# Two of the four weight sums of an FFN pair on GpSimd, joined remainders and re-cut parts in a fast-matrix-product FFN

## The chip, the cores and the metric

The kernel runs on one core of a Trainium2 chip. A core has five engines that run side by side and meet at semaphores: TensorE (PE in the profile; its weight loads are PEld), VectorE (DVE), ScalarE (ACT), GpSimd (POOL) and SyncE (SP), which here starts nearly all transfers. The time is the device time of the whole program in microseconds (us); lower is better.

## The reference, cut to what matters

Two decoder layers run over 1024 prompt tokens and 64 sample tokens (T = 1088), model width 1024. Each layer has three kinds of sequence mixing, an output projection, and the feed-forward part (FFN) that the change is about:

```python
mix = jnp.concatenate([o_gla, o_lru, o_mla], axis=-1) @ w_out
x = _layer_norm(DEEPNORM_ALPHA * x + gate1 * mix, ln1_g, ln1_b)
h2 = x * (1 + scale2) + shift2
g_ff, u_ff = jnp.split(h2 @ ffn_w_gu, 2, axis=-1)     # 1024 -> 2 x 2816
f = (jax.nn.silu(g_ff) * u_ff) @ ffn_w_down           # 2816 -> 1024
x = _layer_norm(DEEPNORM_ALPHA * x + gate2 * f, ln2_g, ln2_b)
```

Everything is float32.

## The kernel before, in words

The kernel is one launch; each stage has an instruction stream for every engine, and the order in each stream is written out by hand (no scheduler moves anything). `stage_out_ffn` holds the output projection, both layer norms and the FFN; it runs once per layer.

**Three passes.** TensorE multiplies in a rounded float32 form. Each operand is split into a rounded part ("hi", cast by ScalarE) and a remainder ("lo" = raw minus hi, subtracted by VectorE), and each product is made of three passes: hi by hi, hi by lo, lo by hi (`three_passes`, lines 434 to 436).

**Pairs and seven products.** A pair `m` is 128 gate and 128 up columns of `w_gu` for one half of the tokens. There are 22 such column blocks and two token halves (512 tokens as 2 x 256, then 576 as 2 x 288), so 44 pairs per layer. A pair is a 2 x 2 block product (two halves of the contraction, two halves of the tokens), made in seven block products instead of eight. For this a weight set has seven slots of 128x512: slots 0, 2, 4 and 5 are loaded by SyncE (`pair_in`, four transfers), and slots 3, 2, 1 and 6 are filled, in this order, by four sums (`w_sum`, lines 2512 to 2525, all on VectorE): slot3 = slot2 + slot5; slot2 = slot0 - slot2; slot1 = slot3 - slot0; slot6 = slot4 - slot1. Two sets take turns. The load of slot s of set m waits until product s of pair m-2 is done. Products go to four PSUM banks in turn (0 to 3); VectorE combines the seven results (`step` in the vector block, lines 2571 to 2625) into gate and up values, ScalarE applies silu, and VectorE multiplies.

**Rounding.** ScalarE rounds slot by slot into a ring of six (`w_rounded`, L2338); VectorE takes the remainder slot by slot, in place (`w_rest`, L2530), five products ahead of TensorE (`LO_AT`). TensorE waits for the remainder before each product.

**Parts.** `FPART` cuts the 22 blocks of a token half into eight parts of two or three pairs, so 16 parts (0 to 15) per layer. After the pairs of a part come its down products (`down`): 8 units of 512 tokens in the first token half, 16 units of 288 in the second, in PSUM banks 4 to 7. A unit sums over the pairs of the part. The first few units (`first`: 2 in the first token half, 4 in the second) are started without the part's last pair; then TensorE waits for the last pair's activations (`s_ul`, line 2253), finishes these units, does the transposes of a layer norm that were hung on this part (`norms_beside`), and then the other units. VectorE adds each unit to the residual stream (L420), takes the remainders of the down weights (L2536), and in the middle of the down phase makes the four sums of one pair ahead (`SUMS_IN_D`) and some remainders (`LO_D`).

The activations of a part's last pair pass a chain over two engines: VectorE adds the last product (L2603), ScalarE applies silu (L2408), VectorE multiplies (L2554), ScalarE rounds (L2353), VectorE takes the remainder (L2548). Its VectorE links stand in one queue with the down weights' remainders and all the rest.

**The last part.** Its down weights come in one transfer, `w_tail` (L2170), which lands in the room of weight set 0 and so waits for all products of the last but one pair. SyncE's queue is in order: for each pair m of a part it issues `pair_in(m + 2)`, and the wait for `w_tail` stands after the pairs of part 14. Part 15 before is the pairs 41, 42 and 43:

```python
for q in range(NQ):
    for m in range(*PAIRS[q]):
        if m + 2 < NPAIR:
            pair_in(m + 2)
    ...
    if q == NQ - 2:
        sp.wait_ge(s_pp, 7 * (NPAIR - 1))
        src = a["w_down"][bass.ds(layer[0], 1), :, :, NF - 3:NF]
        sp.dma_start(WLR, ...).then_inc(s_wt, 16)
```

GpSimd does nothing in this stage.

Of the kernel before, what the change touches and what calls it, by code (L numbers as in the profile page):

```python
# [27 lines left out]
P = 128  # L28
# [94 lines left out]
def build(nc, a, out, n_phys):  # L123
    ctx = ExitStack()
    with ctx:
# [1857 lines left out]
        FPART = [(0, 2), (2, 5), (5, 8), (8, 11), (11, 14), (14, 17), (17, 19), (19, 22)]  # L1983
# [11 lines left out]
        nh, nl = 5, 4  # L1995
        for q, (m0, m1) in enumerate(PAIRS):
            ends = (7 * m1 + 4, 7 * m1 + 2, 7 * m1 + NR) if q < NQ - 1 else (7 * m1,) * 3
            for j in range(7 * m0, 7 * m1):
                h, l_ = max(nh, min(j + 7, ends[0])), max(nl, min(j + 6, ends[1]))
                HI_AT[j], LO_AT[j] = range(nh, h), range(nl, l_)  # L2000
                nh, nl = h, l_
            HI_D[q], LO_D[q] = range(nh, ends[2]), range(nl, ends[2])
            nh = nl = ends[2]
# [22 lines left out]
        WLH = at("w_tail_hi", o, [P, KD, 3, P])  # L2026
# [4 lines left out]
        WLR, WLL = (at("w_tail" + x, r1 + 10 * 4 * 288 * 4, [P, KD, 3, P]) for x in ("", "_lo"))  # L2031
        assert o <= end and o_wo >= r1 + KD * T * 4
        o = o_small
        P1T, U2T, U3T, C22T = (at(x, o + 1152 * i, [P, 288]) for i, x in enumerate(
            ("ffn_p1", "ffn_u2", "ffn_u3", "ffn_c22")))
# [51 lines left out]
        def stage_out_ffn():  # L2087
# [9 lines left out]
            s_ws, s_wh, s_wl = (sem(x) for x in ("w_ffn_sums", "w_ffn_rounded", "w_ffn_rest"))  # L2097
            s_pp, s_p1, s_sa, s_sb = (sem(x) for x in ("ffn_product_done", "p1_kept", "silu_0_done", "silu_1_done"))
            s_u2, s_u3, s_c22, s_u5, s_c11, s_c21, s_c12 = (sem(x) for x in (
                "u2_ready", "u3_ready", "c22_ready", "u5_ready", "c11_ready", "c21_ready", "c12_ready"))  # L2100
            bank_read = (s_p1, s_u2, s_u3, s_u5, s_c11, s_c21, s_c12)
# [21 lines left out]
            with nc.Block() as block:  # L2123
                @block.sync
                def _(sp):
# [33 lines left out]
                    for q in range(NQ):  # L2159
# [18 lines left out]
                def _(pe):  # L2178
# [49 lines left out]
                    def down(q):  # L2228
                        m0, m1 = PAIRS[q]
                        last, first = m1 - m0 - 1, 2 * NU[q] // KD if q < NQ - 1 else 4  # L2230
# [16 lines left out]
                        for u in range(first):  # L2247
# [62 lines left out]
                def _(act):  # L2310
# [17 lines left out]
                    def w_rounded(j):  # L2328
                        m, i = divmod(j, 7)
                        if i in (0, 4, 5):  # L2330
                            act.wait_ge(s_set[m % 2], 64 * (m // 2 + 1))
                        else:
                            act.wait_ge(s_ws, 4 * m + {3: 1, 2: 2, 1: 3, 6: 4}[i])
# [141 lines left out]

                @block.vector
                def _(dve):
# [34 lines left out]
                    def w_sum(m, p):  # L2512
                        w = WGR[:, m % 2]
                        if p == 1:
                            dve.wait_ge(s_set[m % 2], 64 * (m // 2 + 1))
                            ins = dve.tensor_tensor(w[:, 3], w[:, 2], w[:, 5], ALU.add)  # L2516
                        if p == 2:
                            ins = dve.tensor_tensor(w[:, 2], w[:, 0], w[:, 2], ALU.subtract)  # L2518
                        if p == 3:
                            dve.wait_ge(s_ws, 4 * m + 1)  # L2520
                            ins = dve.tensor_tensor(w[:, 1], w[:, 3], w[:, 0], ALU.subtract)  # L2521
                        if p == 4:
                            dve.wait_ge(s_ws, 4 * m + 3)
# [3 lines left out]
                    def w_rest(j):  # L2527
                        m, i = divmod(j, 7)
                        dve.wait_ge(s_wh, j + 1)
                        dve.tensor_tensor(WGL[:, m % 2, i].bitcast(F32R), WGR[:, m % 2, i], WGH[:, (j + 1) % NR],  # L2530
                                          ALU.subtract).then_inc(s_wl, 1)
# [12 lines left out]
                    def act_rest(m, h):  # L2544
# [4 lines left out]
                                          ALU.subtract).then_inc(s_ul, 1)  # L2549

# [20 lines left out]
                    def step(m, i):  # L2571
# [5 lines left out]
                        u1, u2, u3, c22 = (v[:, 0:w] for v in (P1T, U2T, U3T, C22T))  # L2577
# [4 lines left out]
                        if i == 1:  # L2582
# [4 lines left out]
                            if m > m0:  # L2587
                                act_rest(m - 1, 0)
                                act_rest(m - 1, 1)
# [426 lines left out]
```

## Time and profile before

| | us |
|---|---|
| median of 3 runs (lowest, highest) | 3690.62 (3680.36, 3694.93) |
| profiled execution | 3688.22 |
| its span, first to last instruction | 3686.4 |
| TensorE busy | 3321.2 (90%) |
| VectorE busy | 2378.9 (65%) |
| ScalarE busy | 1538.3 (42%) |
| GpSimd busy | 193.7 (5%) |

The profile is of one execution. The time is 1.8 us more than the span (start and end outside the first and last instruction). "Idle before" and the arrow name how long an engine stood still before an instruction and what released it. A busy share is an average over stages with different limits, so the waits are read stage by stage. PEclk is the granted TensorE clock: 1.00 is 2.4 GHz, 0.50 is 1.2 GHz, and a value between is a stretch with some of both.

### The profile page before, as it was taken

Reading aid. Unit: us, or ns where it says so; the run is one execution under the profiler, and the core shown is the slowest. Engines: PE = TensorE matmul, PEld = TensorE weight load, DVE = VectorE, ACT = ScalarE, POOL = GpSimd, SP = SyncE. Lnnn points to the kernel's source line nnn. Section 1 sums busy time; section 2 is a strip of 40 time slices with the busy share of each in tenths; the row PEclk is TensorE's granted clock in tenths of the full one; section 3 lists DMA queues with packets and bytes.
Section 4 is the critical chain, followed back from the end, with each engine's and each line's share of the span. In section 5 each row is a group of like instructions: output and inputs, shape, how many; then the busy total and the mean of one; then the engine's idle time right before and its main releaser. Section 6 shows DMA issues by size and latency. Waiting matters only on the chain. (4 is left out here: it accounts for less than half of the span.)

```text
span 3686.4 us, 61020 instructions
## 1 busy us (share of the span) xinstructions
PE 3321.2 (90%) x23548; PEld 2773.6 (75%) x23548; DVE 2378.9 (65%) x4902; ACT 1538.3 (42%) x3093; POOL 193.7 (5%) x252
## 2 busy tenths in 40 slices
PE   6987899998989998999789869999989999989996
PEld 5864566666988888999779546666668888789996
DVE  5146664444688879888642466644447877898886
ACT  5235554443344444453231545634424444544331
POOL 0011111110000000000000121011100000000000
PEclk9987998998999999999989869999989999999998
DMA  5144003442123322222111500044312332222221
GB/s 205 31 151 144 22 1 134 153 161 58 48 84 89 90 86 75 83 85 87 36 51 29 190 29 1 1 182 162 115 46 65 90 95 81 83 79 87 84 93 55
DMA packets 157570, 316.86 MB, mean 86 GB/s; under 512 B 18491, under 2 KB 85341, under 8 KB 146406
## 3 DMA queue, kind: packets, MB, share of 16 engines
q1 hardware_dynamic: 145766, 229.08, 20.1%
q0 software_dynamic: 11520, 83.89, 6.4%
q8 instruction: 191, 3.13, 0.4%
q14 instruction: 93, 0.76, 0.1%
HBM read 306.41 MB, written 6.51 MB: 85 GB/s over the span
## 5 line engine op out<-in xcount | busy, mean ns | idle before, releaser
L2338 ACT CAST w_ffn_hi<-w_ffn 128x512 fp32r<-128x512 f32 x616 | 367.8, 617 | 312.8 <-DVE w_ffn L2521 183.1
L434 PE MATMUL psum<-ffn_act_hi,w_down_hi 128*128 128x288 f32 (+1 forms) x960 | 335.8, 350 | 104.5 <-DVE ffn_act_lo L2548 86.6
L2530 DVE TENSOR_TENSOR w_ffn_lo<-w_ffn,w_ffn_hi 128x512 fp32r<-128x512 f32 x616 | 415.0, 682 | 7.5 <-ACT w_ffn_hi L2338 5.8
L435 PE MATMUL psum<-h_lo,w_ffn_hi 128*128 128x256 f32 (+1 forms) x1408 | 408.7, 290 | 0.0
L434 PE MATMUL psum<-h_forms_hi,w_ffn_hi 128*128 128x288 f32 x1232 | 366.1, 297 | 29.0 <-DVE ffn_u L2596 29.0
L436 PE MATMUL psum<-h_forms_hi,w_ffn_lo 128*128 128x288 f32 x1232 | 365.7, 297 | 0.0
L420 DVE SCALAR_TENSOR_TENSOR xT<-psum,adaT,xT 128x512 f32<-128x512 f32 (+3 forms) x432 | 236.4, 567 | 199.5 <-PE psum L436 199.0
L434 PE MATMUL psum<-h_hi,w_ffn_hi 128*128 128x256 f32 x1232 | 348.3, 283 | 4.3 <-DVE xT L427 1.9
L436 PE MATMUL psum<-h_hi,w_ffn_lo 128*128 128x256 f32 x1232 | 347.9, 282 | 0.0
L436 PE MATMUL psum<-ffn_act_hi,w_down_lo 128*128 128x288 f32 (+1 forms) x960 | 329.3, 343 | 0.0
L435 PE MATMUL psum<-ffn_act_lo,w_down_hi 128*128 128x288 f32 (+1 forms) x960 | 328.5, 342 | 0.0
L434 PEld LDWEIGHTS psum<-ffn_act_hi,w_down_hi 128*128 128x128 f32 x960 | 188.2, 196 | 133.7 <-DVE ffn_act_lo L2548 96.6
L435 PEld LDWEIGHTS psum<-h_lo,w_ffn_hi 128*128 128x128 f32 x1408 | 267.3, 190 | 0.7
L434 PEld LDWEIGHTS psum<-h_forms_hi,w_ffn_hi 128*128 128x128 f32 x1232 | 233.5, 190 | 30.0 <-DVE ffn_u L2596 29.9
L434 PEld LDWEIGHTS psum<-h_hi,w_ffn_hi 128*128 128x128 f32 x1232 | 235.2, 191 | 6.7 <-DVE xT L427 2.3
L436 PEld LDWEIGHTS psum<-h_hi,w_ffn_lo 128*128 128x128 f32 x1232 | 235.1, 191 | 0.0
L436 PEld LDWEIGHTS psum<-h_forms_hi,w_ffn_lo 128*128 128x128 f32 x1232 | 233.6, 190 | 0.0
L436 PEld LDWEIGHTS psum<-ffn_act_hi,w_down_lo 128*128 128x128 f32 x960 | 188.2, 196 | 16.4
L435 PEld LDWEIGHTS psum<-ffn_act_lo,w_down_hi 128*128 128x128 f32 x960 | 188.5, 196 | 13.1
L1883 ACT COPY keysT<-psum 128x512 f32<-128x512 f32 x192 | 106.8, 589 | 202.2 <-PE psum L1793 195.6
L1937 DVE TENSOR_REDUCE dec_max<-psum 128x1 f32<-128x1024 f32 x64 | 78.3, 1224 | 170.3 <-PE psum L1809 170.3
L1663 DVE TENSOR_REDUCE mla_neg_max<-psum 128x1 f32<-128x128 f32 (+7 forms) x128 | 96.7, 756 | 92.8 <-PE psum L1487 92.0
(436 smaller groups left out, 7631.9 us busy)
## 6 DMA issues: line engine op xcount, KB each, us to landing
w_ffn<-in_w_gu SPq DMA_DIRECT2D x352, 256.0 KB, 2.6
w_ada_pair<-in_w_ada SPq DMA_DIRECT2D x40, 1024.0 KB, 5.2
w_down<-in_w_down SPq DMA_DIRECT2D x176, 192.0 KB, 2.4
w_ada_first<-in_w_ada SPq DMA_DIRECT2D x4, 2048.0 KB, 22.0
w_out<-in_w_out SPq DMA_DIRECT2D x16, 512.0 KB, 7.3
w_down<-in_w_down SPq DMA_DIRECT2D x64, 128.0 KB, 2.1
w_in_T<-in_w_in_T SPq DMA_DIRECT2D x12, 512.0 KB, 4.3
z<-in_x_prompt SPq DMA_DIRECT2D x8, 512.0 KB, 6.9
```

The source lines that it names most:

```text
L420: ins = eng.scalar_tensor_tensor(XT[:, c, t0:t0 + wp], ps[:, 0:wp], ADA[:, gate + c, 0:1], XT[:, c, t0:t0 + wp], ALU.mult, ALU.add)
L434: pe.matmul(o, wh, xh, start=first, stop=False)
L435: pe.matmul(o, wh, xl, start=False, stop=False)
L436: return pe.matmul(o, wl, xh, start=False, stop=last)
L1663: dve.tensor_reduce(NM[:, i % 2:i % 2 + 1], bank(2 * (i % 2), 2)[:, 0:scores_item(i)], AX.X, ALU.max, negate=True).then_inc(s_mx, 1)
L1883: copy(dst, src).then_inc(done, 1)
L1937: lk(dve.tensor_reduce(MXD[:, s % 2, :], bank(3, 2), AX.X, ALU.max))
L2338: act.copy(WGH[:, (j + 1) % NR].bitcast(F32R), WGR[:, m % 2, i]).then_inc(s_wh, 1)
L2530: dve.tensor_tensor(WGL[:, m % 2, i].bitcast(F32R), WGR[:, m % 2, i], WGH[:, (j + 1) % NR], ALU.subtract).then_inc(s_wl, 1)
```

## The change

1. **GpSimd takes two of the four sums.** A new GpSimd block makes slot 3 and then slot 2 of every pair as soon as its set has landed; VectorE keeps slots 1 and 6 at their old places.
2. **Joined remainders.** `w_rest` takes two neighbouring slots in one instruction where the ring allows: a pair's seven remainders are four instructions (`LO_GROUPS`), one product later than before. The two halves of an activation's remainder are one instruction (`acts_rest`), except for a part's last pair; two of the seven combining additions are one instruction of twice the width.
3. **Four first units** in every part, where the first token half had two.
4. **The norm's transposes** stand before the wait for the last pair's activations instead of after it.
5. **Parts are cut anew**: the last two of a token half are (17, 20), (20, 22) instead of (17, 19), (19, 22). `w_tail` is for two pairs instead of three.

```diff
-        FPART = [(0, 2), (2, 5), (5, 8), (8, 11), (11, 14), (14, 17), (17, 19), (19, 22)]
+        FPART = [(0, 2), (2, 5), (5, 8), (8, 11), (11, 14), (14, 17), (17, 20), (20, 22)]
...
-        nh, nl = 5, 4
+        LO_GROUPS = [(7 * m + i, 2 if i + 1 + m % 2 < 7 and (i or m % 2) else 1) for m in range(NPAIR)
+                     for i in ((0, 2, 4, 6) if m % 2 else (0, 1, 3, 5))]
+        LO_GROUPS = [(j, min(n, 7 - j % 7)) for j, n in LO_GROUPS]
+        nh, nl = 5, 3
...
-            ends = (7 * m1 + 4, 7 * m1 + 2, 7 * m1 + NR) if q < NQ - 1 else (7 * m1,) * 3
+            ends = (7 * m1 + 4, 7 * m1 + 1, 7 * m1 + NR) if q < NQ - 1 else (7 * m1,) * 3
...
+                while nl < len(LO_GROUPS) and LO_GROUPS[nl][0] < min(j + 5, ends[1]):
+                    nl += 1
+                LO_AT[j] = LO_GROUPS[l0:nl]
...
-                            src = a["w_down"][bass.ds(layer[0], 1), :, :, NF - 3:NF]
+                            src = a["w_down"][bass.ds(layer[0], 1), :, :, NF - 2:NF]
...
-                        last, first = m1 - m0 - 1, 2 * NU[q] // KD if q < NQ - 1 else 4
+                        last, first = m1 - m0 - 1, 4
...
+                        norms_beside(q)
                         pe.wait_ge(s_ul, 2 * m1)
                         for u in range(first):
                             part(u, last).then_inc(s_dn, 1)
-                        norms_beside(q)
...
+                @block.gpsimd
+                def _(pool):
+                    for m in range(NPAIR):
+                        w = WGR[:, m % 2]
+                        pool.wait_ge(s_set[m % 2], 64 * (m // 2 + 1))
+                        pool.tensor_tensor(w[:, 3], w[:, 2], w[:, 5], ALU.add).then_inc(s_wp, 1)
+                        pool.wait_ge(s_wp, 2 * m + 1)
+                        pool.tensor_tensor(w[:, 2], w[:, 0], w[:, 2], ALU.subtract).then_inc(s_wp, 1)
...
                     def w_sum(m, p):
                         w = WGR[:, m % 2]
-                        if p == 1:
-                            dve.wait_ge(s_set[m % 2], 64 * (m // 2 + 1))
-                            ins = dve.tensor_tensor(w[:, 3], w[:, 2], w[:, 5], ALU.add)
-                        if p == 2:
-                            ins = dve.tensor_tensor(w[:, 2], w[:, 0], w[:, 2], ALU.subtract)
                         if p == 3:
-                            dve.wait_ge(s_ws, 4 * m + 1)
+                            dve.wait_ge(s_wp, 2 * m + 1)
                             ins = dve.tensor_tensor(w[:, 1], w[:, 3], w[:, 0], ALU.subtract)
...
-                    def w_rest(j):
+                    def w_rest(j, n):
                         m, i = divmod(j, 7)
-                        dve.wait_ge(s_wh, j + 1)
...
+                        r = (j + 1) % NR
+                        dve.wait_ge(s_wh, j + n)
+                        dve.wait_ge(s_wp, 2 * m + 2)
+                        if i <= 1 < i + n or i <= 4 < i + n:
+                            dve.wait_ge(s_ws, 2 * m + 2)
+                        dve.tensor_tensor(WGL[:, m % 2, i:i + n].bitcast(F32R), WGR[:, m % 2, i:i + n], WGH[:, r:r + n],
+                                          ALU.subtract).then_inc(s_wl, n)
...
+                    def acts_rest(m):
...
+                        dve.tensor_tensor(UL[:, f, v].bitcast(F32R), UR[:, f, v], UH[:, f, v], ALU.subtract).then_inc(s_ul, 2)
...
-                            dve.tensor_tensor(c22, p, u3, ALU.add).then_inc(s_c22, 1)
-                            dve.tensor_tensor(u2, p, u2, ALU.add).then_inc(s_u5, 1)
+                            dve.tensor_tensor(UTS[:, 2:4, 0:w], p.unsqueeze(1).to_broadcast([P, 2, w]), UTS[:, 1:4:2, 0:w],
+                                              ALU.add).then_inc(s_c22, 1)
```

## Rows read from the trace of the kernel before

**Rows 1.** The page: busy us, share of the span, instructions; granted clock in 40 slices.
```profile
PE 3321.2 (90%) x23548; PEld 2773.6 (75%) x23548; DVE 2378.9 (65%) x4902; ACT 1538.3 (42%) x3093; POOL 193.7 (5%) x252
PEclk9987998998999999999989869999989999999998
```

**Rows 2.** TensorE's waits: engine line <- releaser: us in total, times, longest.
```profile
PE psum L434 <- DVE ffn_act_lo L2548: 88.8, 32, 4.8
PE psum L434 <- DVE ffn_u L2596: 30.3, 6, 13.4
PE psum L434 <- DVE xT L420: 12.9, 9, 2.2
```

**Rows 3.** Timelines of SP, DVE and PE near layer 0's end: start, us, instruction [idle before].
```profile
1792.10 0.38 SPq L2170 DMA_DIRECT2D w_tail<-in_w_down  x1
1792.53 2.15 SPq L2135 DMA_DIRECT2D w_ffn<-in_w_gu  x4
...
1801.42 0.69 DVE L2516 TENSOR_TENSOR w_ffn<-w_ffn 128x512 f32<-128x512 f32 x1 [15.13 <-DMA w_ffn<-in_w_gu]
...
1805.43 0.61 PE L434 MATMUL psum<-h_forms_hi,w_ffn_hi 128*128 128x288 f32 x1 [13.36 <-DVE ffn_u L2596]
```

**Rows 4.** Stretches: us, busy (instructions) of PE, PEld, DVE, ACT, POOL, clock, DMA.
```profile
1805.40:1809.00 3.60, 3.57 (x15) 3.57 (x16) 3.55 (x8) 2.18 (x5) 0.00 (x0) 0.50 0.00 0
1809.00:1813.00 4.00, 4.00 (x26) 4.00 (x26) 3.13 (x8) 3.12 (x6) 0.00 (x0) 0.80 0.00 0
...
1077.10:1082.10 5.00, 4.96 (x24) 4.26 (x25) 2.52 (x4) 0.82 (x1) 0.00 (x0) 0.69 0.26 79
...
1287.90:1292.90 5.00, 5.00 (x18) 3.14 (x18) 1.50 (x2) 1.50 (x3) 0.00 (x0) 0.66 0.28 79
...
1601.80:1605.40 3.60, 3.60 (x30) 3.60 (x31) 2.37 (x8) 1.29 (x2) 0.00 (x0) 1.00 0.29 78
```

**Rows 5.** PE's timeline: first unit and end of the wait, parts 4 and 12.
```profile
1228.32 0.40 PE L434 MATMUL psum<-ffn_act_hi,w_down_hi 128*128 128x512 f32 x1
...
1234.37 0.80 PE L434 MATMUL psum<-ffn_act_hi,w_down_hi 128*128 128x512 f32 x1 [3.14 <-DVE ffn_act_lo L2548]
...
1653.07 0.29 PE L434 MATMUL psum<-ffn_act_hi,w_down_hi 128*128 128x288 f32 x1
...
1658.10 0.40 PE L434 MATMUL psum<-ffn_act_hi,w_down_hi 128*128 128x288 f32 x1 [1.68 <-DVE ffn_act_lo L2548]
```

**Rows 6.** DVE's timeline in part 4: its last long idle time, the chain's last link.
```profile
1211.42 0.42 DVE L2586 TENSOR_TENSOR ffn_u<-psum,ffn_p 128x256 f32<-128x256 f32 x1 [0.80 <-PE psum L436]
1211.76 0.75 DVE L2548 TENSOR_TENSOR ffn_act_lo<-ffn_act,ffn_act_hi 128x256 fp32r<-128x256 f32 x2
...
1233.88 0.43 DVE L2548 TENSOR_TENSOR ffn_act_lo<-ffn_act,ffn_act_hi 128x256 fp32r<-128x256 f32 x1 [0.47 <-ACT ffn_act_hi L2353]
```

**Rows 7.** DVE's groups by form: shapes, count | busy us, mean ns | idle before.
```profile
L2530 DVE TENSOR_TENSOR w_ffn_lo<-w_ffn,w_ffn_hi 128x512 fp32r<-128x512 f32 x616 | 415.0, 682 | 7.5 <-ACT w_ffn_hi L2338 5.8
L2672 DVE TENSOR_TENSOR w_out_lo<-w_out,w_out_hi 128x1024 fp32r<-128x1024 f32 x16 | 19.5, 1218 | 11.0 <-ACT w_out_hi L2421 11.0
L2586 DVE TENSOR_TENSOR ffn_u<-psum,ffn_p 128x256 f32<-128x256 f32 x44 | 18.5, 421 | 29.5 <-PE psum L436 29.5
```

**Rows 8.** GpSimd's additions by line: ns min/median/max; then timelines of POOL and DVE.
```profile
L855 POOL TENSOR_TENSOR hT<-lru_i,hT x4: 2491/2512/2535, 252.9 to 2077.6; 128x1088 f32<-128x1088 f32 x4
L860 POOL TENSOR_TENSOR gv_gg<-gv_gg,gla_norm_g x8: 1389/1395/1850, 334.7 to 2154.9; 128x576 f32<-128x576 f32 x8
...
338.80 1.84 POOL L860 TENSOR_TENSOR gv_gg<-gv_gg,gla_norm_g 128x576 f32<-128x576 f32 x1
...
338.20 1.18 DVE L1206 TENSOR_TENSOR gla_sample_states<-gla_sample_states,gla_chunk_decay 128x512 f32<-128x512 f32 x1 [4.60 <-ACT gla_state_blocks L1052]
339.41 0.69 DVE L1207 TENSOR_TENSOR gla_sample_states<-gla_sample_states,psum 128x512 f32<-128x512 f32 x1
```

**Rows 9.** The page's DMA issues: KB each, median us to landing.
```profile
w_ffn<-in_w_gu SPq DMA_DIRECT2D x352, 256.0 KB, 2.6
```

**Rows 10.** The tile w_tail: DVE's row (ns min/median/max), and its landing.
```profile
L2542 DVE TENSOR_TENSOR w_tail_lo<-w_tail,w_tail_hi x4: 1748/1749/1751, 1816.4 to 3638.2; 128x1536 fp32r<-128x1536 f32 x4
...
DMA to landing us min/median/max: 6.6/6.6/6.6
```

**Rows 11.** PE's timeline: the first product of layer 0's pair 23.
```profile
1414.39 0.40 PE L434 MATMUL psum<-h_forms_hi,w_ffn_hi 128*128 128x288 f32 x1 [1.16 <-DVE ffn_u L2596]
```

More of the change, by code:

```diff
@@ L1994, in build @@
         HI_AT, LO_AT, HI_D, LO_D = {}, {}, {}, {}
-        nh, nl = 5, 4
+        LO_GROUPS = [(7 * m + i, 2 if i + 1 + m % 2 < 7 and (i or m % 2) else 1) for m in range(NPAIR)
+                     for i in ((0, 2, 4, 6) if m % 2 else (0, 1, 3, 5))]
+        LO_GROUPS = [(j, min(n, 7 - j % 7)) for j, n in LO_GROUPS]
+        nh, nl = 5, 3
         for q, (m0, m1) in enumerate(PAIRS):
-            ends = (7 * m1 + 4, 7 * m1 + 2, 7 * m1 + NR) if q < NQ - 1 else (7 * m1,) * 3
+            ends = (7 * m1 + 4, 7 * m1 + 1, 7 * m1 + NR) if q < NQ - 1 else (7 * m1,) * 3
             for j in range(7 * m0, 7 * m1):
[L1999 to L2003, printed above, removed]
+                h = max(nh, min(j + 7, ends[0]))
+                HI_AT[j], nh = range(nh, h), h
+                l0 = nl
+                while nl < len(LO_GROUPS) and LO_GROUPS[nl][0] < min(j + 5, ends[1]):
+                    nl += 1
+                LO_AT[j] = LO_GROUPS[l0:nl]
+            l0 = nl
+            while nl < len(LO_GROUPS) and sum(LO_GROUPS[nl]) <= ends[2]:
+                nl += 1
+            HI_D[q], LO_D[q] = range(nh, ends[2]), LO_GROUPS[l0:nl]
+            nh = ends[2]
         SUMS_IN_D = [q for q in range(NQ - 1) if q != NQ // 2 - 1]
@@ L2030, in build @@
         UH = at("ffn_act_hi", o, [P, 3, NB1]); o += 3 * NB1 * 4
-        WLR, WLL = (at("w_tail" + x, r1 + 10 * 4 * 288 * 4, [P, KD, 3, P]) for x in ("", "_lo"))
+        WLR, WLL = (at("w_tail" + x, r1 + 10 * 4 * 288 * 4, [P, KD, 2, P]) for x in ("", "_lo"))
         assert o <= end and o_wo >= r1 + KD * T * 4
         o = o_small
-        P1T, U2T, U3T, C22T = (at(x, o + 1152 * i, [P, 288]) for i, x in enumerate(
-            ("ffn_p1", "ffn_u2", "ffn_u3", "ffn_c22")))
+        UTS = at("ffn_u", o, [P, 4, 288])
+        P1T, U3T, C22T, U2T = (UTS[:, i] for i in range(4))
         assert o + 5 * 1152 <= r1
@@ L2576, in step @@
                         p = bank(j % 4)[:, 0:w]
-                        u1, u2, u3, c22 = (v[:, 0:w] for v in (P1T, U2T, U3T, C22T))
+                        u1, u2, u3 = (v[:, 0:w] for v in (P1T, U2T, U3T))
                         if i == 0 and m > m0:
@@ L2587, in step @@
                             if m > m0:
[L2588 to L2589 removed]
+                                acts_rest(m - 1)
                         if i == 2:
@@ L2700, in _ @@
                         if u == 13:
-                            for p in range(1, 5):
-                                w_sum(0, p)
+                            w_sum(0, 3)
+                            w_sum(0, 4)
                         if u in (14, 15):
-                            w_rest(2 * (u - 14))
-                            w_rest(2 * (u - 14) + 1)
+                            w_rest(*LO_GROUPS[u - 14])
                     form_rest(0, 4)
+                    w_rest(*LO_GROUPS[2])
                     form_rest(0, 5)
```

40 lines of the change are left out of this document (21 added, 19 removed).

## The prediction, as it stood before the changed kernel ran

> **What bounds the kernel now.** I read the page first: TensorE is busy for 3321 of 3686 us [rows 1], so the change can win only TensorE's idle time in the FFN and what the slower clock behind idle time costs. Next the waits of TensorE [rows 2]: 88.8 us in 32 waits for the remainder of the activations (L2548), one per part, and 30.3 us in 6 waits for L2596, of which one is 13.4 us. That one I followed through the queues near the end of layer 0 [rows 3]. SyncE issues `w_tail` at 1792.10 and only then the four loads of pair 43: its queue is in order, and the wait for pair 42's last product stands ahead of them. VectorE stands 15.13 us for that set, TensorE 13.36 us. The 6 waits for L2596 hold this one twice (26.7 us). After it the clock is 0.50 for 3.6 us and 0.80 for 4.0 us [rows 4]: 0.50 x 3.6 + 0.20 x 4.0 = 2.6 us of work lost.
>
> The other waits are one per part. In part 4 the down phase begins at 1228.32 and TensorE stands 3.14 us until 1234.37 [rows 5], 6.05 us after the start. I call this distance the chain. Its length is VectorE's backlog: VectorE has its last long idle time before 1211.42 and works almost without a break until the last remainder at 1233.88 [rows 6]. Behind a 3.1 us wait the clock reads 0.69 and 0.66 over 5 us [rows 4] (parts 1 and 5, first and last of five alike ones), some 1.7 us of work lost each. In part 12 the chain is 5.03 us and the wait 1.68 us [rows 5]; behind a wait of that size the clock stays 1.00 [rows 4].
>
> **The tail order.** The new cut makes part 14 the pairs 39 to 41, so `pair_in(43)` is queued ahead of the wait for `w_tail`. This takes away 13.4 + 2.6 = 16.0 us per layer. `w_tail` now has one pair (11.2 us; seven products of 1.6) to land and be split in. It took 6.6 us to land beside four loads with 1.5 MB [rows 10], is now 1 MB, and its two remainders shrink from 1.75 us to 1.22, the row for 128x1024 [rows 7, 10]. It fits. But the last part has two pairs: its early units hold one pair instead of two, and cover about 1.7 us less of a chain that is 4.2 us today and perhaps 3.5 then. I give back 1.0 us. Part 14, with two pairs, stands 2.6 and 1.1 us today; with three it becomes like part 12: I take 1.9 saved. Sum 16.9 us per layer.
>
> **What VectorE loses and gains.** In its stream an instruction starts some 0.08 us before its predecessor's record ends, so 128x512 costs 0.60, 128x1024 1.14 and 128x256 0.33 us [rows 7]. Two sums less: 1.20 us per pair. Three joined remainders: 3 x 0.07; joined additions and activation remainders: 0.07 each. Together 1.55 us per pair. The middle and the last pair of a part decide the backlog: 3.1 us, and one remainder is due later.
>
> Against it stands GpSimd. No row shows its sum at 128x512; 1088 columns take 2.51 and 576 take 1.39 us [rows 8], so 2.2 ns per column and 1.25 us for 512 by that line (an estimate; ends 0.6, VectorE's own pace, and 2.5, the long row). The two engines also stand in each other's way: VectorE's L1206 of 128x512 with both inputs in SBUF took 1.18 us beside a GpSimd addition, not the 0.68 of such a form, and the GpSimd addition that overlapped it took 1.84 instead of 1.39; L1207 with an input in PSUM took 0.69 at the same time [rows 7, 8]. So one seems to wait until the other's whole instruction is done, unless VectorE reads PSUM.
>
> The Trainium skill says the same (SBUF — State Buffer, the overview of its two sides): the pair of ports is an exclusive lock, held for the whole instruction, against VectorE operations with two SBUF inputs. It speaks against this change; the trace agrees in the three rows named.
>
> When does it strike? Set m+1's last load is issued when product 5 of pair m-1 is done, 1.4 us before that pair's end, and lands 2.6 us later [rows 9]: 1.3 us into pair m, and for a part's last pair 1.3 us into the chain. GpSimd then runs 1.25 us, takes its own semaphore, and runs 1.25 us again. About 74% of VectorE's stream has two SBUF inputs, so each addition holds it 0.9 us or so, at worst 1.25. I laid the stream of the middle and last pair of part 4 out instruction by instruction. Middle pair: 1.3 us held (VectorE idles at first), its last addition ends 0.3 us earlier than today. Last pair: 2.1 us held. In the chain: two more, 2.1 us. Sum +5.5 - 3.1 - about 0.8 for remainders moved or not due = +1.5: the chain becomes 7.5 us instead of 6.05. The ends: 4.0 if GpSimd costs nothing, 9.5 if its additions hold VectorE longer.
>
> **Four first units and transposes ahead.** In the first token half two units with two pairs cover 2.9 us (1228.32 to 1231.23); four cover 5.8 us. The transposes ahead add 1.0 to 2.9 us (8 to 16 of them; parts 0 to 6 have some). Parts 1 to 5 cover 6.9 to 8.7 us against a chain of 7.5: the wait goes and with it the slow clock, 3.14 + 1.7 = 4.8 us each. What is late next is a remainder: slot 6 of an odd last pair now stands behind the sums of the next set and ends about 0.5 us after TensorE could use it. I keep 0.8 us: 5 x 4.0 = 20.0 us per layer. The other early units' conditions (a free bank, the split down weights) come in time: VectorE idles 7 us of part 3's down phase today, and has 1.35 us less to do there.
>
> Part 0 covers 5 to 6 us of a chain of 6.4 today: of 4.8 + 1.9 us waits and 2 us of slow clock 3.0 are saved. Parts 6 and 7: part 6 becomes like part 5. Part 7 has now two pairs, and behind it VectorE forms the block sums of the next token half, some 29 us without a break from the chain's end to pair 23's start at 1414.39 [rows 11]. VectorE sets this stretch, so down work moved out of it (5.8 us of TensorE) moves from under cover to the open. Its chain is about 7.8 us (7.4 today) with 2.9 covered. Part 6's wait of 3.3 us and slow clock of 3.1 gained, this lost, 1.8 us gained on VectorE: 3.7 us saved in both.
>
> **Second token half.** There first is four already. Part 12 covers 3.35 us; laid out the same way, the chain goes from 5.0 to 5.7 us, the wait from 1.7 to 2.4: 0.7 us lost each in parts 12 and 13. Parts 9 to 11 have transposes (1.0 to 1.9 us) as new cover: 1.0 us won each; in layer 1 VectorE is without a break after the chain, and it is the two sums less (1.2 us) that win it. Part 8: nothing, a longer chain against 2 us more cover. Together +1.6 us.
>
> **Sum.** 16.9 + 20.0 + 3.0 + 3.7 + 1.6 = 45.2 us per layer, 90.4 in both. The profiled execution took 3688.2: 3597.8. It lies 2.4 us under the median of the runs shown, so I forecast **3600 us** (-2.4%).
>
> **The rivals.**
> *GpSimd's additions hold VectorE about 2 us per part longer than laid out* (chain 9.5 us). For it: in each later pair both sets of instructions want the same ports, and 1.25 us is a line through two points. Against: the rows show waits of 0.5 us, never a pile. Parts 1 to 5 then stand 1 to 2.5 us, some clock lost: 12 of 20 us gone; parts 0, 6, 7: 4; second half, seven parts x 1.4: 10. Per layer 45 - 26 = 19: 3600 + 52 = 3652. Chance 0.20.
> *GpSimd costs VectorE hardly anything* (it slips into idle time or PSUM reads, chain 4 to 5 us). Then the second half's waits fall to about 0.5 us and parts 0 and 7 win 1.5 each: 11 us more per layer, 3578. Chance 0.14.
> *`w_tail` comes late now.* It has half the cover it had. If ScalarE stands in its queue for it and the chain of the last part waits behind, 5 us per layer: 3610. For it: ScalarE's rounding of it comes at product 3, 6.4 us after the issue, and 6.6 is the landing. Chance 0.10.
> *Slower than before*: VectorE is the pace of every pair. Per pair of 10.0 us it has 8.2 + 0.8 (down weights) and two holds. If one holds it 2.5 us, the upper end, its stream is 14 us and TensorE waits in the products too (for L2530 and L2592), in every part. It decides from 3 us plus clock in each of 15 parts, 45 us per layer, which is where a hold costs some 1.6 us instead of 0.9. At 1.25 us more each of six holds per part adds 7.5 us less 3 of cover or slack, 15 parts, two layers, 135 us: 3735. Chance 0.03.
> The forecast itself has 0.53.
>
> **How the numbers follow.** The tail order alone is worth 32 us and rests on one queue. The low end takes the cheap GpSimd and a little (3574), the high end the expensive one (3655); what lies outside is part of the 0.03, the tails of the two and some error of my layout, under 0.2. The likeliest case alone spans 3585 to 3620. A measurement of this kernel tells about 0.5% (18 us) from nothing. Faster 0.94, the same 0.03, slower 0.03.
>
> **What would show it.** TensorE's 13.4 us wait for L2596 is gone in both layers, and SyncE issues pair 43's loads ahead of `w_tail`. The wait for L2548 falls from 88.8 to about 40 us, all of it in parts 0, 7 and the second half; behind parts 1 to 5 the clock reads 1.00. GpSimd has 176 additions of 1.25 us where alone and up to 2.4 beside VectorE; some L2530-like rows of VectorE have maxima 1.2 us above their median, those reading PSUM do not. The prediction is wrong if TensorE waits for the remainders inside the products, if GpSimd's additions take well over 2 us each, or if the waits in parts 1 to 5 only became shorter.

## The result, and the profile after

| | before | changed |
|---|---|---|
| median, lowest and highest (us) | 3690.84 (3680.36, 3694.93) | 3651.02 (3644.46, 3654.12) |
| profiled execution | 3688.2 | 3649.7 |

Four executions of each. The ratio is 0.9894, with a 95% interval of 0.9869 to 0.9919: the change wins 1.1%, some 39 us, where 90 were forecast (2.4%). The time lies near the top of the range and on the first rival's figure (3652).

The page of the changed kernel, busy time and granted clock; it answers to [rows 1]:

```profile
PE 3309.3 (91%) x23548; PEld 2760.5 (76%) x23548; DVE 2384.5 (65%) x4318; ACT 1542.5 (42%) x3093; POOL 463.2 (13%) x428
PEclk9997999998999999999989969999989999999998
```

VectorE has 584 instructions fewer than before and lost two sums per pair, yet it is busy for 5.6 us more. That is the first sign of the cost.

TensorE's waits, to be read beside [rows 2] (waited-for line, us in total, times, longest):

```profile
PE psum L434 <- DVE ffn_act_lo L2565: 34.9, 16, 3.6
PE psum L434 <- DVE w_down_lo L2553: 23.9, 12, 3.3
PE psum L434 <- DVE w_ffn_lo L2547: 20.9, 36, 1.1
...
PE psum L434 <- DVE xT L420: 8.5, 10, 2.3
PE psum L308 <- DVE ffn_u L2626: 7.6, 4, 2.9
PE psum L256 <- DVE ffn_u L2626: 6.0, 4, 2.4
PE psum L319 <- DVE ffn_u L2626: 3.6, 3, 1.9
```

The two waits of 13.4 us for the last pair's first combination are gone, and the activations' wait fell from 88.8 to 34.9 us. Three kinds are new or far larger: down-weight remainders (4.9 us before, all in 4 waits), pair-weight remainders inside the products (none before), and the norm's transposes, which now stand ahead of the activations' wait and themselves wait for VectorE's last addition (17.2 us; none before). [rows 2] and the 4.9 us make 137 us; the seven rows above make 105. In the old places 88.6 us were won (53.9, 30.3 and 4.4), and 57.1 of them came back as 20.9 + 19.0 + 17.2 in the three new ones.

The chain in part 12, the place of [rows 5]'s last two rows: timelines of PE, POOL and DVE (start, us, instruction, idle before).

```profile
1644.55 0.30 PE L434 MATMUL psum<-ffn_act_hi,w_down_hi 128*128 128x288 f32 x1
...
1651.23 0.40 PE L434 MATMUL psum<-ffn_act_hi,w_down_hi 128*128 128x288 f32 x1 [3.33 <-DVE ffn_act_lo L2565]
```

```profile
1645.28 1.66 POOL L2490 TENSOR_TENSOR w_ffn<-w_ffn 128x512 f32<-128x512 f32 x1 [9.11 <-DMA w_ffn<-in_w_gu]
1647.02 1.38 POOL L2492 TENSOR_TENSOR w_ffn<-w_ffn 128x512 f32<-128x512 f32 x1
```

```profile
1645.71 0.45 DVE L2623 TENSOR_TENSOR ffn_u<-psum,ffn_u 128x288 f32<-128x288 f32 x1
1646.26 1.00 DVE L2637 TENSOR_TENSOR ffn_act<-ffn_u 128x288 f32<-128x288 f32 x1
1647.18 1.63 DVE L2553 TENSOR_TENSOR w_down_lo<-w_down,w_down_hi 128x384 fp32r<-128x384 f32 x1
1648.73 0.45 DVE L2626 TENSOR_TENSOR ffn_u<-psum,ffn_u 128x288 f32<-128x288 f32 x1
...
1650.71 0.46 DVE L2565 TENSOR_TENSOR ffn_act_lo<-ffn_act,ffn_act_hi 128x288 fp32r<-128x288 f32 x1 [0.50 <-ACT ffn_act_hi L2362]
```

The chain is 6.68 us, not 5.03. GpSimd's two additions fall into it. Each holds one VectorE instruction that reads two SBUF tensors: L2637 takes 1.00 where the same shape at L2577 takes 0.46, and a down-weight remainder takes 1.63 where it takes 0.55 just before. The additions with an input in PSUM (L2623, L2626) keep their 0.45. Behind the wait the clock is no longer 1.00 [rows 4], while in parts 2 to 5, where the wait is gone or short, it now is. In part 1 it is not: TensorE stands 2.75 us for a down weight there, and the clock behind that reads 0.66 (stretches in parts 12, 1, 2 and 4; the columns of [rows 4]):

```profile
1651.20:1655.20 4.00, 3.97 (x21) 3.97 (x22) 2.38 (x8) 0.46 (x1) 0.00 (x0) 0.67 0.33 88
1085.30:1090.30 5.00, 5.00 (x15) 3.96 (x16) 4.68 (x8) 2.27 (x5) 0.00 (x0) 0.66 0.06 10
1130.40:1135.40 5.00, 5.00 (x26) 4.04 (x25) 2.77 (x5) 2.69 (x7) 0.00 (x0) 1.00 0.40 110
1230.20:1235.20 5.00, 4.99 (x21) 3.87 (x21) 3.56 (x8) 1.47 (x3) 0.00 (x0) 1.00 0.53 154
```

All instructions of the stage show the same selection: weight remainders, GpSimd's two lines, one combining addition and one activation product (ns min/median/max).

```profile
L2547 DVE TENSOR_TENSOR w_ffn_lo<-w_ffn,w_ffn_hi x352: 677/1215/2345, 991.9 to 3598.2; 128x1024 fp32r<-128x1024 f32 x132, 128x512 fp32r<-128x512 f32 x44
L2490 POOL TENSOR_TENSOR w_ffn<-w_ffn x88: 1268/1360/2332, 981.1 to 3558.6; 128x512 f32<-128x512 f32 x88
L2492 POOL TENSOR_TENSOR w_ffn<-w_ffn x88: 1291/1393/2306, 983.0 to 3560.0; 128x512 f32<-128x512 f32 x88
...
L2609 DVE TENSOR_TENSOR ffn_u<-psum,ffn_u x88: 410/434/460, 1001.5 to 3596.2; 128x256 f32<-128x256 f32 x44, 128x288 f32<-128x288 f32 x44
...
L2577 DVE TENSOR_TENSOR ffn_act<-ffn_u x88: 412/459/1589, 1012.9 to 3605.7; 128x256 f32<-128x256 f32 x44, 128x288 f32<-128x288 f32 x44
```

The added time is in the maxima; L2609, which reads PSUM, has none.

### The profile page after: what moved, and what is told of

Read it like the earlier page. It is cut to its first block and busy times, and to the rows that moved or that the text cites. A ratio compares the mean times of both kernels' runs of the same rounds, so it can differ in the third digit from the quotient of the medians.

```text
span 3647.9 us, 61284 instructions
## 1 busy us (share of the span) xinstructions
PE 3309.3 (91%) x23548; PEld 2760.5 (76%) x23548; DVE 2384.5 (65%) x4318; ACT 1542.5 (42%) x3093; POOL 463.2 (13%) x428
## 5 line engine op out<-in xcount | busy, mean ns | idle before, releaser
L2547 DVE TENSOR_TENSOR w_ffn_lo<-w_ffn,w_ffn_hi 128x1024 fp32r<-128x1024 f32 (+1 forms) x352 | 409.4, 1163 | 15.6 <-issue 11.9
L434 PE MATMUL psum<-ffn_act_hi,w_down_hi 128*128 128x288 f32 (+1 forms) x992 | 344.5, 347 | 64.1 <-DVE ffn_act_lo L2565 31.7
L436 PE MATMUL psum<-ffn_act_hi,w_down_lo 128*128 128x288 f32 (+1 forms) x992 | 337.7, 340 | 0.0
L435 PE MATMUL psum<-ffn_act_lo,w_down_hi 128*128 128x288 f32 (+1 forms) x992 | 337.3, 340 | 0.0
L2490 POOL TENSOR_TENSOR w_ffn<-w_ffn 128x512 f32<-128x512 f32 x88 | 129.8, 1475 | 1585.3 <-DMA w_ffn<-in_w_gu 1585.3
L434 PEld LDWEIGHTS psum<-ffn_act_hi,w_down_hi 128*128 128x128 f32 x992 | 196.0, 198 | 91.6 <-DVE ffn_act_lo L2565 36.7
L435 PEld LDWEIGHTS psum<-ffn_act_lo,w_down_hi 128*128 128x128 f32 x992 | 196.3, 198 | 13.5
```

The costliest lines, as they stand in the source:

```text
L434: pe.matmul(o, wh, xh, start=first, stop=False)
L435: pe.matmul(o, wh, xl, start=False, stop=False)
L436: return pe.matmul(o, wl, xh, start=False, stop=last)
L2490: pool.tensor_tensor(w[:, 3], w[:, 2], w[:, 5], ALU.add).then_inc(s_wp, 1)
L2547: dve.tensor_tensor(WGL[:, m % 2, i:i + n].bitcast(F32R), WGR[:, m % 2, i:i + n], WGH[:, r:r + n], ALU.subtract).then_inc(s_wl, n)
```

## The experiments

Kernels of one group ran on one chip beside the kernel before (its medians: 3689.67, 3689.65, 3685.16). Ratios are against it, with 95% intervals; differences between two experiments are differences of medians, and I call one resolved only where the ratios' intervals are apart. The changed kernel ran in a session of its own, and the base of the second group (3617.70) is a kernel of the first, so where chips differ the ratios are the better measure.

### First group: which part of the change wins, which costs

**All four sums back on VectorE, the rest as changed.**

```diff
-  @block.gpsimd ...
+  if p == 1: dve.tensor_tensor(w[:, 3], w[:, 2], w[:, 5], ALU.add)
+  if p == 2: dve.tensor_tensor(w[:, 2], w[:, 0], w[:, 2], ALU.subtract)
```

> The change with all four sums back on VectorE at their old places; joined remainders, four first units, transposes ahead and the new cut stay. Theory H (holds): in the changed kernel GpSimd's additions hold VectorE 0.8 us each, three pairs of them fall into the chain of each part, and only two pairs of sums leave it. Then the chain of part 12 falls from 6.6 by 3 x 1.6 and rises by 2 x 1.2, to about 4.3 us, its wait from 3.3 to about 1.0, and the kernel is faster than the changed one: 3610 to 3625 us. Rival R (relief): taking two sums off VectorE is worth its price and what was lost is due to the joined, later remainders and the four first units; then this is slower than the changed kernel, 3660 us or more, and the waits inside the products grow.

Measured: 3621.56 (3620.54 to 3625.18), 0.9823 (0.9806 to 0.9839). Faster than the change, by 29 us: in this kernel the two sums are worth more on VectorE than on GpSimd where the change starts them. The time is as expected, its path only in part: part 12 waits 1.85 us, not 1.0, and its chain is 5.19 us, not 4.3. Only the pair of holds inside the chain shows in its length, not three pairs.

```profile
PE 3296.2 (91%) x23548; PEld 2747.5 (76%) x23548; DVE 2350.5 (65%) x4494; ACT 1542.4 (43%) x3093; POOL 194.1 (5%) x252
```

This line gives the price of a hold. VectorE has 176 instructions more than in the changed kernel, its lines 2525 and 2528:

```profile
L2525 DVE TENSOR_TENSOR w_ffn<-w_ffn x88: 679/682/689, 991.2 to 3545.3; 128x512 f32<-128x512 f32 x88
L2528 DVE TENSOR_TENSOR w_ffn<-w_ffn x88: 682/684/690, 991.8 to 3545.9; 128x512 f32<-128x512 f32 x88
```

A record is 0.68 us long but starts 0.08 us before the one ahead of it ends, so in VectorE's stream a sum costs 0.60 us, by the prediction's own reading: 106 us for the 176. Without them VectorE would be busy for 2245 us; with GpSimd's additions beside it, it is busy for 2384.5: 140 us for 176 additions, **0.79 us each**. The longer means of the stretched rows, shape by shape, add up to about the same (136 us). So moving a sum cost VectorE 0.19 us more than it saved, 34 us in all.

**The new cut alone**, on the kernel before.

```diff
-  (14, 17), (17, 19), (19, 22)]      w_tail: 3 pairs
+  (14, 17), (17, 20), (20, 22)]      w_tail: 2 pairs
```

> The kernel before with nothing but the new cut of the parts (17, 20), (20, 22) and the last transfer for two pairs. Both theories: the 13.4 us wait of each layer and the slow clock behind it go (32 us), part 7 and the last part cover less: 3658 to 3664 us. If the gain of the whole change over the kernel before (40 us) is nearly all this, the other edits together brought less than 10 us.

Measured: 3662.89 (3660.33 to 3667.34), 0.9933 (0.9916 to 0.9949): 27 us, two thirds of what the whole change wins. The 13 us waits are gone, the activations' wait is not touched:

```profile
PE psum L434 <- DVE ffn_act_lo L2548: 90.5, 32, 5.8
...
PE psum L434 <- DVE ffn_u L2596: 4.0, 4, 1.4
```

**GpSimd's sums alone**, on the kernel before (the GpSimd block of the diff, VectorE keeps slots 1 and 6, remainders slot by slot).

> The kernel before with nothing but two of the four sums on GpSimd. Theory H: each part's chain grows by 3 x 1.6 - 2 x 1.2 = 2.4 us, uncovered here, in some 30 parts, and the slow clock comes into the second token half: 60 to 100 us slower than before, 3750 to 3790. Rival R: the chain shrinks by 1 to 2 us, 30 to 50 us faster, 3640 to 3660.

Measured: 3749.36 (3741.27 to 3758.57), 1.0160 (1.0142 to 1.0177): 60 us **slower**, at the low end of what was expected. Alone, this part of the change is a loss:

```profile
PE psum L434 <- DVE ffn_act_lo L2555: 138.2, 32, 6.0
```

The same 32 waits as before, 1.5 us longer each, where 2.4 was expected. In the full change the same additions cost 29 us (the experiment above), about half; that the cut and the longer cover hide the rest is my reading, no run separates it.

**GpSimd's sums after the chain.** In a part's down phase GpSimd waits until the last pair's activations are done.

```diff
   pool.wait_ge(s_set[m % 2], 64 * (m // 2 + 1))
+  if m - 1 in [m1 for _, m1 in PAIRS[:-1]]:
+      pool.wait_ge(s_ul, 2 * (m - 1))
```

> The changed kernel, but GpSimd waits, for the set that lands during a part's chain, until the chain's last link is done. Theory H: one pair of holds (1.6 us) leaves the chain of every part and falls into the down phase where VectorE has slack: part 12 waits 1.7 instead of 3.3 us, the slow clock behind it goes; 20 to 35 us faster than the changed kernel, 3615 to 3630. Rival R: no change within 8 us, or slower where the down phase is VectorE's.

Measured: 3617.70 (3609.91 to 3621.22), 0.9813 (0.9797 to 0.9830): 33 us faster than the change. One wait per part gives back what GpSimd cost, and VectorE is busy for 2349.8 us, no longer than with the sums at home (2350.5). Part 12 shows what left the chain:

```profile
1629.80 0.29 PE L434 MATMUL psum<-ffn_act_hi,w_down_hi 128*128 128x288 f32 x1
...
1634.97 0.40 PE L434 MATMUL psum<-ffn_act_hi,w_down_hi 128*128 128x288 f32 x1 [1.82 <-DVE ffn_act_lo L2567]
```

The chain is 5.17 us, and the clock over the 4 us behind the wait reads 1.00 again. Against all four sums on VectorE the intervals overlap: on its own, GpSimd's help is worth nothing that these runs can tell. The remaining waits:

```profile
PE psum L434 <- DVE ffn_act_lo L2567: 22.4, 14, 2.6
PE psum L434 <- DVE w_down_lo L2555: 22.1, 12, 3.3
PE psum L434 <- DVE w_ffn_lo L2549: 21.2, 37, 1.1
```

The activations' wait fell by a third, and the other two did not move. So GpSimd is not their cause; the second group asks for it, with this kernel as its base.

### Second group: the waits that GpSimd does not explain

The pair-weight wait has two forms. Layer 0 has 20 of them. Seven are for a single remainder, slot 6 of an odd pair. DVE and PE in part 2 of the changed kernel:

```profile
1121.07 0.68 DVE L2534 TENSOR_TENSOR w_ffn<-w_ffn 128x512 f32<-128x512 f32 x1
1121.78 0.69 DVE L2537 TENSOR_TENSOR w_ffn<-w_ffn 128x512 f32<-128x512 f32 x1
1122.39 0.69 DVE L2547 TENSOR_TENSOR w_ffn_lo<-w_ffn,w_ffn_hi 128x512 fp32r<-128x512 f32 x1
```

```profile
1123.22 0.36 PE L434 MATMUL psum<-h_hi,w_ffn_hi 128*128 128x256 f32 x1 [0.60 <-DVE w_ffn_lo L2547]
```

The remainder that TensorE needs stands behind the next pair's two sums, of which nothing is due. These seven waits are 0.25 to 0.60 us. The other thirteen are for joined remainders, up to 1.12 us, and in twelve of them a held instruction stands just ahead in VectorE's queue. The same part, 3 us earlier:

```profile
1115.32 1.51 DVE L2637 TENSOR_TENSOR ffn_act<-ffn_u 128x256 f32<-128x256 f32 x1
1116.76 0.41 DVE L2626 TENSOR_TENSOR ffn_u<-psum,ffn_u 128x256 f32<-128x256 f32 x1
1117.65 0.62 DVE L2577 TENSOR_TENSOR ffn_act<-ffn_u 128x256 f32<-128x256 f32 x1 [0.48 <-ACT ffn_u L2417]
1118.20 1.21 DVE L2547 TENSOR_TENSOR w_ffn_lo<-w_ffn,w_ffn_hi 128x1024 fp32r<-128x1024 f32 x1
```

```profile
1119.56 0.36 PE L434 MATMUL psum<-h_hi,w_ffn_hi 128*128 128x256 f32 x1 [0.62 <-DVE w_ffn_lo L2547]
```

In the kernel with all sums on VectorE layer 0 has nine such waits up to part 8: six of the single kind, now 0.6 to 1.7 us, since four sums stand ahead instead of two, and three joined ones in the first pairs of a token half. None of these has a held instruction ahead.

The down-weight wait is a queue on two engines. ACT in part 1, then DVE, then PE:

```profile
1082.78 0.29 ACT L342 ACTIVATE ln_std<-mean_var,eps 128x1 f32<-128x1 f32 x1 [1.11 <-DVE mean_var L328]
1083.01 1.20 ACT L349 ACTIVATE hT<-psum,ln_std,ln_rstd 128x1024 f32<-128x1024 f32 x1
1084.11 0.50 ACT L2352 CAST w_down_hi<-w_down 128x384 fp32r<-128x384 f32 x1
```

```profile
1084.64 0.56 DVE L2553 TENSOR_TENSOR w_down_lo<-w_down,w_down_hi 128x384 fp32r<-128x384 f32 x1 [0.49 <-ACT w_down_hi L2352]
```

```profile
1085.26 0.50 PE L434 MATMUL psum<-ffn_act_hi,w_down_hi 128*128 128x512 f32 x1 [2.75 <-DVE w_down_lo L2553]
```

ScalarE waits for a norm's statistics, makes its rows, and only then rounds the down weight that TensorE stands for. Parts 0, 1 and 4 are of this kind. In part 7, with four such waits (5.7 us in all), there is no norm: the block sums of the next token half and their rounding stand in the two queues.

**Remainder before the sums.**

```diff
-  w_sum(m + 1, 3); w_sum(m + 1, 4)      # at product 2
   for g in LO_AT[j]: w_rest(*g)
+  w_sum(m + 1, 3); w_sum(m + 1, 4)
```

> Base: the changed kernel with GpSimd after the chain (3618 us). One edit: at product 2 VectorE takes the remainder that is due before the two sums of the next pair, not after them. Theory: part of what was lost is that the remainders are one product later and stand behind the sums; TensorE's waits inside the products for L2547 (37 waits, 21 us in the base) lose those of 0.6 us at the last product of odd pairs: 3 to 8 us faster than the base, 3610 to 3615. Rival: those waits only take the place of waits for the chain; no change within 2 us.

Measured: 3609.96 (3603.61 to 3614.90), 0.9781 (0.9758 to 0.9803); 8 us under the base, the intervals just touch. The pair-weight wait goes from 21.2 (37 times) to 14.9 us (23 times): the single kind is gone, and of the thirteen joined waits in layer 0 eleven are left.

**Remainders slot by slot again, one product earlier**, as in the kernel before.

```diff
-  LO_GROUPS = [(7 * m + i, 2 if ...)]; nh, nl = 5, 3;  ... min(j + 5, ends[1])
+  LO_GROUPS = [(j, 1) for j in range(7 * NPAIR)]; nh, nl = 5, 4;  ... min(j + 6, ends[1])
```

> Same base. The remainders one slot at a time and one product earlier again, as before the change; all else stays. Theory: the joining saves 0.2 us of VectorE per pair and costs waits inside the products; the waits for L2547 (21 us) fall under 5 us and the kernel is 8 to 15 us faster than the base, 3603 to 3610. Rival: joined instructions are fewer chances for GpSimd to hold VectorE and are worth having; then 5 to 15 us slower.

Measured: 3596.79 (3594.12 to 3600.75), 0.9753 (0.9732 to 0.9775): 21 us under the base, resolved. It did better than I expected. Of TensorE's waits for VectorE's remainders in the FFN two kinds are left:

```profile
PE psum L434 <- DVE w_down_lo L2553: 22.6, 12, 3.2
PE psum L434 <- DVE ffn_act_lo L2565: 21.7, 15, 2.6
```

with no row for the pair weights. GpSimd's additions are where they were and still hold VectorE (a single remainder takes up to 1825 ns, median 682), and VectorE is even busy for 24 us more than in the base (2373.7 against 2349.8), but nothing waits for a pair's weights. The joined instruction saves 0.07 us three times a pair [rows 7]; it is ready only when its second slot is, and is asked for a product later, so that one hold ahead of it makes TensorE wait. The edit takes both back at once; how much is the joining and how much the product of lead, no run separates.

**Down weights first.** ScalarE rounds down weights 5 and 6 ahead of the norm's root and rows; VectorE takes the remainder of weight 5 ahead of the norm's scales (parts 0, 1, 4).

```diff
+  down_rounded(q, NW); down_rounded(q, NW + 1)
   norms_beside(q, 0)
...
+  if q in LN1_AT: down_rest(q, NW)
```

> Same base. ScalarE rounds down weights 5 and 6 of a part ahead of the norm's roots and rows, and VectorE takes the remainder of down weight 5 between the statistics and the scales in the parts with first-norm rows (0, 1, 4). Theory: with four first units the sixth unit's weights are late since their slot is free only when unit 0 ends, and behind that the norm's work stands in both queues; TensorE's waits for w_down_lo (12 waits, 22 us) fall by 1 to 2 us in six parts: 5 to 10 us faster, 3608 to 3613. Rival: the transfer itself is late; under 2 us.

Measured: 3608.26 (3599.79 to 3608.97), 0.9783 (0.9762 to 0.9803): 9 us under the base, as expected in size, the intervals just touching; the down-weight wait falls from 22.1 to 16.4 us.

**Two first units in the first token half**, as before.

```diff
-  last, first = m1 - m0 - 1, 4
+  last, first = m1 - m0 - 1, 2 * NU[q] // KD if q < NQ - 1 else 4
```

> Same base. Two first units in the first token half again, as before; the transposes stay ahead of the wait. Theory: the waits for w_down_lo (22 us) go, but parts 0 to 7 cover 2.9 us less of a chain of 6 to 7 us, so the waits for the activations' remainder come back at 1 to 3 us with the slow clock behind some: between no change and 20 us slower, 3618 to 3638. Rival: four first units bring nothing once GpSimd is out of the chain, and this is faster.

Measured: 3624.27 (3619.46 to 3630.25), 0.9828 (0.9804 to 0.9852): 7 us over the base, not resolved. The trace shows why it is little: the activations' wait rises from 22.4 to 30.4 us, and the down weights' falls from 22.1 to 12.1. Four units ask for down weight 5 that much sooner.

### Third group: together, and the kind of GpSimd work

**The three repairs together** (GpSimd after the chain, remainders slot by slot, down weights first).

> The three repairs together: GpSimd after the chain, remainders one slot at a time and one product earlier, down weights ahead of the norm's work. Alone the last two gave some 21 and 10 us on the same base (3618). Theory: they repair different waits (L2547 in the products, w_down_lo in the down phase) and add up: 3585 to 3592 us. Rival: the same VectorE backlog stands behind both, and the second only uncovers the next wait: 3594 to 3600.

Measured: 3591.06 (3579.53 to 3598.47), 0.9750 (0.9733 to 0.9766). It has the lowest median of all, 60 us under the changed kernel; by the ratios, which take out the difference of the chips, it is some 53. The median lies in the first expectation, at its upper end, but the four executions reach from 3580 to 3598, and the ratio is only 0.0003 lower than that of the slot-by-slot kernel. So that the repairs add up is not shown.

**The same with all sums on VectorE** (no GpSimd).

> As the kernel with the three repairs, but all four sums on VectorE and GpSimd idle. Theory: with GpSimd out of the chain its additions are worth having, for VectorE is busy with 1.2 us of sums per pair in exchange for holds that now partly fall into slack; sums on VectorE are 5 to 15 us slower than the repaired kernel. Rival: a hold costs as much as a sum saves (two holds 1.6, two sums 1.2 us), so there is no difference beyond 4 us, and GpSimd brings nothing.

Measured: 3600.76 (3596.84 to 3602.81), 0.9766 (0.9749 to 0.9782). 10 us by the medians for GpSimd (6 by the ratios), in the expected direction, but the intervals overlap, and the rival is not excluded. Its down-weight wait is 28.0 us in 30 waits against 18.7 in 18.

**The norm's transposes after the wait**, on the base of the second group.

```diff
-  norms_beside(q)
   pe.wait_ge(s_ul, 2 * m1)
   for u in range(first): part(u, last)
+  norms_beside(q)
```

> Base: the changed kernel with GpSimd after the chain (3618 us). The norm's transposes stand behind the first units' last parts again, as before the change. Theory: the transposes ahead are cover in eleven parts: parts 1 to 6 stand up to 1 us more, parts 8 to 11 1 to 2 us, and the slow clock returns behind some, but the down weights' wait in parts 0, 1 and 4 shrinks by the 2 us of transposes that stand ahead of it then: together 5 to 15 us slower, 3623 to 3633. Rival: no difference.

Measured: 3628.73 (3621.94 to 3638.23), 0.9851 (0.9829 to 0.9873): 11 us over the base, the intervals just touching. The activations' wait doubles:

```profile
PE psum L434 <- DVE ffn_act_lo L2567: 43.5, 26, 2.9
```

So the transposes are a cover, worth about half of the 21 us that they take off this wait (11 us by the medians, 14 by the ratios).

**GpSimd busy as long, but reading nothing.** All sums are on VectorE (the first experiment), and GpSimd writes a scratch tile eight times when a set has landed. The writes are extra work.

```diff
+  pool.wait_ge(s_set[m % 2], 64 * (m // 2 + 1))
+  for _ in range(8): lp(pool.memset(SCR, 0.0))      # 128x288
```

> The changed kernel with all four sums on VectorE (3622 us), and GpSimd filling a small scratch tile eight times per pair when a set has landed: it is busy for 2.5 to 3 us there as in the changed kernel, but reads nothing; the fills leave nothing that is used. Theory: what holds VectorE is the shared way of reading SBUF, so fills that only write hold little: within 6 us of the kernel without them, and VectorE's two-input rows stay at their medians. Rival: any GpSimd access holds a VectorE instruction with two SBUF inputs: 25 to 60 us slower, 3645 to 3680.

Measured: 3618.37 (3612.78 to 3623.35), 0.9815 (0.9798 to 0.9831), the same as without them (0.9823). GpSimd's group (busy us, mean ns, idle before), then two of VectorE's with two SBUF inputs:

```profile
L2492 POOL MEMSET scratch<- 128x288 f32 x704 | 238.5, 339 | 1600.4 <-DMA w_ffn<-in_w_gu 1565.0
```

```profile
L2584 DVE TENSOR_TENSOR ffn_act<-ffn_u x88: 417/439/461, 1008.7 to 3576.2; 128x256 f32<-128x256 f32 x44, 128x288 f32<-128x288 f32 x44
L2579 DVE TENSOR_TENSOR ffn_act_lo<-ffn_act,ffn_act_hi x56: 679/721/762, 1010.5 to 3567.1; 128x512 fp32r<-128x512 f32 x28, 128x576 fp32r<-128x576 f32 x28
```

238 us of GpSimd work from the same moments on stretch nothing: 461 is the largest of 88, where the changed kernel had 1589 (L2577), and VectorE is busy for 2350.8 us, as without the fills (2350.5). What holds VectorE is that GpSimd reads SBUF tensors, not that it is busy. The rule of the Trainium skill (SBUF — State Buffer, the overview of its two sides) draws the line there: the lock is against a GpSimd operation that reads SBUF. These runs agree: the additions stretched L2577 to 1589 ns, the fills left it at 461.

## Why the prediction was wrong

**Right: the tail.** Both 13.4 us waits went; the cut alone won 27 us, with its effect on parts 6 and 7 in it, against 33.8 forecast for the tail order and parts 14 and 15. SyncE issues pair 43's loads ahead of `w_tail`, which goes out at 1796.05. In layer 0 the last part's chain is 3.18 us (3.5 forecast), its own wait 1.6 us.

**Right: the mechanism of a hold, and nearly its size.** Forecast 0.9 us per addition, on rows with two SBUF inputs alone; measured 0.79. GpSimd's additions were forecast at 1.25 us alone and up to 2.4; the lines show 1.27 and 2.33.

**Right in the main: the activations' wait in parts 1 to 5.** It is gone there (0.8 us is left in layer 0, in part 3, whose chain is 7.8 us where 7.5 was laid out), and its total was forecast at about 40 us: 34.9. The clock reads 1.00 in parts 2 to 5. Part 1 of layer 0 won next to nothing: 3.14 us with the slow clock behind became 2.75 us, for a down weight, with the slow clock behind.

**Wrong: what the relief of VectorE was to take off the chain (3.1 us, and "about 0.8 for remainders moved or not due"), and with it the chain of 5.7 us in part 12.** The two holds inside the chain came, 0.5 and 1.1 us, no more than was laid out (2.1), and so did the two of the last pair ahead of it (1.1 us each). But the chain is 6.7 us and the wait 3.3, not 2.4. The step that failed is the relief: with 2.1 us of holds in the chain and a chain only 0.7 us longer, the forecast took 1.4 us off for what happens ahead of it. The runs show none of that. Part 12's chain is 5.03 us before, 5.19 in the changed kernel with all four sums on VectorE, and 5.17 with two sums gone and GpSimd behind the chain; only what falls into the chain itself made it 6.68. So the premise that VectorE's load in a part's last two pairs sets the chain does not hold in this part. Why the relief is lost there stays open. In parts 13 and 14 the wait is 3.5 and 3.3, and behind it the clock falls (0.67 over 4 us in each, 1.3 us of work), which I had not priced. In parts 8 to 11 the transposes ahead were to be a cover and are themselves held up by the chain, since they wait for VectorE's last addition (17.2 us, with parts 0 and 3). Putting GpSimd behind the chain gave back 33 us, the largest of the three repairs.

**Wrong: "what is late next is a remainder: slot 6", 0.8 us per part.** Slot 6 came as forecast, 0.25 to 0.60 us, seven times in layer 0. What I missed are the thirteen waits for joined remainders beside them, twelve behind a held instruction: 20.9 us in both layers for the two kinds. Remainders slot by slot, a product earlier, won 21 us. I counted what joining saves VectorE (0.07 us each) and not that a joined remainder is ready later and comes with a product less of lead; without both, the same holds made TensorE wait for none. The prediction had named TensorE's waits for remainders inside the products as a sign that it is wrong.

**Wrong: "(a free bank, the split down weights) come in time".** I looked at part 3, whose down phase has VectorE idle for 7 us. In parts 0, 1 and 4 four first units reach down weight 5 while ScalarE and VectorE still do the first norm, in part 7 while they form and round the block sums of the next token half. 23.9 us instead of 4.9; setting these weights first in the parts other than 7 won 9 us, which the intervals hardly separate from nothing.

The waits alone make up most of the 50 us that the forecast had too much. Pair weights: 20.9 us where 8 were allowed (0.8 in ten parts); down weights: 23.9 where the 4.9 of before were to stay; transposes: 17.2 where nothing was put; against that 5 us less for the activations. Together 44. The rest is in the clock and in small terms, which I did not separate; the mean granted clock was 0.940 before, 0.950 after and 0.955 with all three repairs. The repairs one by one are worth 33, 21 and 9 us, together 60. These are not shares of the 50: the forecast had counted the holds in the chain, which the first repair takes out, and the causes overlap, for a hold also stands ahead of most joined remainders that come late.

**The rivals.** The one whose figure was met (3652) said that GpSimd's additions hold VectorE longer than laid out, with losses in every part. That its figure was met is luck in good part: the holds were no longer than laid out, part 3's chain was 7.8 us and not 9.5, parts 1 to 5 did not stand behind the chain, and of the 60 us that the three repairs win, 27 (23 by the ratios) come on top of moving GpSimd's start. The rival on the other side (VectorE as the pace of every pair, from 1.6 us per hold) did not come about in the change; but GpSimd's part alone is a loss, at 0.8 us per hold, since there the 32 waits for the activations grew with the chain. `w_tail` came a little late for ScalarE, which stood 2.1 us for it in layer 0, but this did not lengthen the last part's chain.

## What to carry to other kernels

Before work is moved from VectorE to GpSimd, take off what GpSimd's reads hold VectorE: here a sum of 0.60 us moved away and 0.79 came back. With its start behind the part's chain the loss was gone, but a gain over the sums at home was not resolved (3618 against 3622 us, and 3591 against 3601). An instruction joined out of two is due when its first half is and ready when its second is; count what TensorE may then wait beside what VectorE saves. When a wait is covered with work from further down, ask of each covering instruction what it needs, and look at the busiest part, not the quietest: the cover here waited for weights and for additions behind the same backlog.

## What the runs showed of the hardware

- The hold goes both ways: GpSimd's additions of 128x512 range from 1.27 to 2.33 us beside VectorE, VectorE's remainders of 128x1024 from 1.22 (without GpSimd 1227 ns is their longest) to 2.35 us.
- GpSimd's writes that read no tensor did not hold VectorE: 704 of them, 0.34 us each, and VectorE busy for 2350.8 us beside 2350.5.
- Work taken off an engine can leave it busier: VectorE 2384.5 us with two sums a pair moved away, 2350.5 with them at home.
